# Page loads of a decoder step: one register load per four pages, page groups dealt 3:3:2 over three queues

## The reference, cut to what matters

```python
def dsa_sample(q, k, v, qi, ki, wi, cache_k, cache_v, cache_kidx, page_table, layer):
    ki_past = cache_kidx[layer, page_table].reshape(B, past, IDX_DIM)     # 8 x 32 pages of 128 x 64
    score = indexer_scores(qi, wi, concat([ki_past, ki], 1))              # sum_h w_h * relu(q_h . k)
    score = where(arange(L) <= pos_q, score, -inf)
    _, idx = lax.top_k(score, 256)
    ks, vs = rows idx of cache_k / cache_v by page_table, or of the new k / v   # pages of 128 x 2 x 64
    return sparse_attend(q, ks, vs, idx <= pos_q)                         # softmax over the kept keys
```

## Time and profile before

| What | us |
|---|---|
| median of 3 runs | 3424.85 |
| the profiled execution itself | 3424.24 |
| its span, first to last instruction | 3422.6 |
| index stage, first to last page transpose (L1911) | 1475.6 to 1560.7 |
| sample attention, first key transpose (L2531) to the last value matmul (L2586) | 2099.0 to 2334.9 |
| PE busy over the span | 2926.7 (86%) |
| POOL busy over the span | 315.7 (9%) |

### The profile page before, as it was taken

How to read it: one execution, slowest core, us unless ns; L and a number is a source line. 1 busy time by engine, 2 the same in 40 slices (tenths; PEclk the granted TensorE clock), 3 DMA queues, 4 the chain that set the end, 5 groups by cost and what they waited for, 6 DMA issues and landing times. The chain is left out here.

```text
span 3422.6 us, 45282 instructions
## 1 busy us (share of the span) xinstructions
PE 2926.7 (86%) x17508; PEld 2637.4 (77%) x17508; DVE 1499.2 (44%) x2239; ACT 871.9 (25%) x1350; POOL 315.7 (9%) x502
## 2 busy tenths in 40 slices
PE   7999999998599999677775686766969999999986
PEld 6999999998397899535775353446859999999984
DVE  3323233322545788357775674331342222233325
ACT  2111111110314577113443343321131111111102
POOL 0000000000000000043222003551000000000000
PEclk8999999999799999579998797888979999999998
DMA  3111111110121222142001003543011111111101
GB/s 116 38 50 38 45 42 43 37 49 6 54 66 38 64 70 89 52 108 53 27 24 60 35 1 87 150 130 121 12 58 41 43 43 44 44 44 38 46 10 53
DMA packets 258005, 185.86 MB, mean 54 GB/s; under 512 B 60191, under 2 KB 236527, under 8 KB 257814
## 3 DMA queue, kind: packets, MB, share of 16 engines
q1 hardware_dynamic: 216630, 115.07, 11.8%
q0 software_dynamic: 22752, 61.87, 5.5%
q10 hardware_dynamic: 18432, 6.30, 0.7%
HBM read 156.96 MB, written 26.22 MB: 54 GB/s over the span
## 5 line engine op out<-in xcount | busy, mean ns | idle before, releaser
L310 DVE TENSOR_TENSOR ffn_hidden<-ffn_hidden,ffn_ps_b 128x1092 f32<-128x1092 f32 x44 | 56.9, 1292 | 406.2 <-PE ffn_ps_b L84 406.2
L293 DVE TENSOR_TENSOR ffn_lo_g<-ffn_raw_g,ffn_hi_g 128x1024 fp32r<-128x1024 f32 x44 | 53.9, 1225 | 344.5 <-ACT ffn_hi_g L258 344.5
L177 POOL DMA_DIRECT2D ffn_raw_d<-in_ffn_w_down x44 | 23.5, 533 | 1783.3 <-DVE ffn_lo_d L299 1576.6
L265 ACT ACTIVATE ffn_hi_d<-ffn_raw_d 128x1024 fp32r<-128x1024 f32 x44 | 46.5, 1058 | 549.0 <-PE ffn_ps_b L84 424.6
L280 ACT ACTIVATE ffn_h_hi<-ffn_hidden 128x1092 fp32r<-128x1092 f32 x44 | 49.2, 1119 | 502.4 <-DVE ffn_hidden L310 502.4
L84 PE MATMUL ffn_ps_a<-mixer_mix_hi,ffn_hi_g 128*128 128x364 f32 x528 | 118.9, 334 | 42.6 <-DVE ffn_lo_g L293 30.1
L84 PE MATMUL ffn_ps_a<-ffn_h_hi,ffn_hi_d 128*128 128x364 f32 x528 | 120.2, 337 | 22.6 <-DVE ffn_lo_d L299 18.1
L84 PE MATMUL ffn_ps_a<-first_x_hi,ffn_hi_g 128*128 128x364 f32 x528 | 118.5, 333 | 21.4 <-DVE first_res L322 12.5
L273 ACT ACTIVATE ffn_hidden<-ffn_ps_a 128x1092 f32<-128x1092 f32 x44 | 47.7, 1083 | 316.9 <-PE ffn_ps_a L84 316.9
L84 PEld LDWEIGHTS ffn_ps_a<-mixer_mix_hi,ffn_hi_g 128*128 128x128 f32 x528 | 92.1, 190 | 45.9 <-DVE ffn_lo_g L293 30.6
L84 PE MATMUL ffn_ps_a<-ffn_h_hi,ffn_lo_d 128*128 128x364 f32 x528 | 118.3, 332 | 0.0
(11 more groups left out here) (566 smaller groups left out, 7139.5 us busy)
## 6 DMA issues: line engine op xcount, KB each, us to landing
ffn_raw_g<-in_ffn_w_gate SPq DMA_DIRECT2D x44, 512.0 KB, 3.7
ffn_raw_u<-in_ffn_w_up SPq DMA_DIRECT2D x44, 512.0 KB, 3.7
ffn_raw_d<-in_ffn_w_down POOLq DMA_DIRECT2D x44, 512.0 KB, 3.7
proj_raw<-in_w_in SPq DMA_DIRECT2D x22, 512.0 KB, 3.8
ats_k_raw<-in_cache_k POOLq DMA_DIRECT2D x128, 64.0 KB, 2.2
ats_v_raw<-in_cache_v POOLq DMA_DIRECT2D x128, 64.0 KB, 2.1
scratch_qkv<-proj_stage POOLq DMA_DIRECT2D x12, 544.0 KB, 3.0
delta_cur<-scratch_qkv SPq DMA_DIRECT2D x8, 768.0 KB, 5.4
```

The costliest lines, as they stand in the source:

```text
L177: eng.dma_start(dst, src).then_inc(raw_in[kind], 16)
L265: act.activation(d_hi[:, k, :], raw["d"][:, :], ACT.Copy).then_inc(whi_done["d"], 1)
L293: dve.tensor_tensor(lo[kind][:, :], raw[kind][:, :], hi[kind][:, :].bitcast(F32), ALU.subtract).then_inc(wlo_done[kind], 1)
L310: dve.tensor_tensor(hid, hid, ps_b[:, :, 0:SL], ALU.mult).then_inc(mul_done, 1)
```

## The change

`load_page` becomes `load_pages`: one register load brings the numbers of the four pages of one sample in a step, and four DMAs follow, all from one engine. What one engine loads is therefore a group of four pages, two groups to a step. In the index stage the groups go round SP, POOL, ACT (22, 21 and 21 of 64). In the attention the table `owner` repeats every four steps, shifted by one step for the values; over four steps, keys and values together, SP and POOL load six groups each and ACT four. PE waits only for engines that load into the buffer at hand. Data, buffers, sizes of the DMAs and the computation stay as they are.

```diff
-def load_page(eng, cache, pages, slot, dst, sem):
-    page = eng.value_load(pages[0:1, bass.ds(slot, 1)])
-    eng.dma_start(dst, cache[0, bass.ds(page, 1)].rearrange("o p ... -> (o p) ...")).then_inc(sem, 16)
+def load_pages(nc, eng, engine, cache, pages, slot, dst, sem):
+    _, numbers = nc.values_load_multi_w_load_instructions(pages[0:1, slot:slot + 4], engines=(engine,))
+    for g, page in enumerate(numbers):
+        eng.dma_start(dst(g), cache[0, bass.ds(page, 1)].rearrange("o p ... -> (o p) ...")).then_inc(sem, 16)
...
-    parts = {"sp": [(0, 0), (0, 1), (0, 2)], "pool": [(0, 3), (1, 0), (1, 1)], "act": [(1, 2), (1, 3)]}
+    turns = ("sp", "pool", "act")
...
-            if n >= bufs:
+            mine = [b2 for b2 in range(2) if turns[(2 * n + b2) % 3] == who]
+            if mine and n >= bufs:
                 eng.wait_ge(s["turned"], n - bufs + 1)
-            for b2, g in parts[who]:
-                load_page(eng, cache_kidx, pages, (p * 2 + b2) * PAGES + (i + h * rows_i) * 4 + g,
-                          raw[:, n % bufs, g, b2 * HD:(b2 + 1) * HD], s[f"raw_in_{who}{n % bufs}"])
+            for b2 in mine:
+                load_pages(nc, eng, engine, cache_kidx, pages, (p * 2 + b2) * PAGES + (i + h * rows_i) * 4,
+                           lambda g: raw[:, n % bufs, g, b2 * HD:(b2 + 1) * HD], s[f"raw_in_{who}{n % bufs}"])
...
-    parts = {"sp": [(0, 0), (0, 1), (0, 2)], "pool": [(1, 0), (1, 1), (1, 2), (1, 3)], "act": [(0, 3)]}
+    owner = {0: ("sp", "sp", "act", "sp"), 1: ("act", "pool", "pool", "pool")}
...
-        def load_k(eng, who, n):
+        def load_k(eng, engine, who, n):
+            mine = [b2 for b2 in range(2) if owner[b2][n % 4] == who]
...
-        def load_v(eng, who, m):
+        def load_v(eng, engine, who, m):
+            mine = [b2 for b2 in range(2) if owner[b2][(m + 1) % 4] == who]
```

More of the change, by code:

```diff
@@ L1871, in index_sample, with load_step @@
         block = ctx.enter_context(nc.Block())
-        def load_step(eng, who, n):
+        def load_step(eng, engine, who, n):
             i, p, h = steps[n]
-            if n >= bufs:
+            mine = [b2 for b2 in range(2) if turns[(2 * n + b2) % 3] == who]
+            if mine and n >= bufs:
                 eng.wait_ge(s["turned"], n - bufs + 1)
-            for b2, g in parts[who]:
-                load_page(eng, cache_kidx, pages, (p * 2 + b2) * PAGES + (i + h * rows_i) * 4 + g,
-                          raw[:, n % bufs, g, b2 * HD:(b2 + 1) * HD], s[f"raw_in_{who}{n % bufs}"])
+            for b2 in mine:
+                load_pages(nc, eng, engine, cache_kidx, pages, (p * 2 + b2) * PAGES + (i + h * rows_i) * 4,
+                           lambda g: raw[:, n % bufs, g, b2 * HD:(b2 + 1) * HD], s[f"raw_in_{who}{n % bufs}"])
         @block.sync
@@ L1883, in _ @@
             for n in range(total_steps):
-                load_step(sp, "sp", n)
+                load_step(sp, mybir.EngineType.SP, "sp", n)
         @block.gpsimd
@@ L1888, in _ @@
             for n in range(total_steps):
-                load_step(pool, "pool", n)
+                load_step(pool, mybir.EngineType.Pool, "pool", n)
         @block.tensor
@@ L1905, in turn @@
             def turn(n):
-                for who, which in parts.items():
-                    pe.wait_ge(s[f"raw_in_{who}{n % bufs}"], (n // bufs + 1) * 16 * len(which))
+                for who in turns:
+                    groups = [b2 for m in range(n % bufs, n + 1, bufs) for b2 in range(2)
+                              if turns[(2 * m + b2) % 3] == who]
+                    if groups:
+                        pe.wait_ge(s[f"raw_in_{who}{n % bufs}"], len(groups) * 64)
                 if n >= 2:
@@ L1957, in _ @@
             for n in range(bufs):
-                load_step(act, "act", n)
+                load_step(act, mybir.EngineType.Activation, "act", n)
             act.wait_ge(s["new_dotted"], 1)
@@ L1968, in _ @@
                 if n + bufs < total_steps:
-                    load_step(act, "act", n + bufs)
+                    load_step(act, mybir.EngineType.Activation, "act", n + bufs)
                 if n in cut_at:
@@ L2475, in half @@
             return slice(b2 * HD, (b2 + 1) * HD)
-        def load_k(eng, who, n):
-            if n >= bufs:
+        def load_k(eng, engine, who, n):
+            p, c = divmod(n, chunks)
+            mine = [b2 for b2 in range(2) if owner[b2][n % 4] == who]
+            if mine and n >= bufs:
                 eng.wait_ge(s["turned1"], n - bufs + 1)
[L2480 to L2483, removed]
@@ L2485, in load_v @@
-        def load_v(eng, who, m):
-            if m >= bufs:
-                eng.wait_ge(s["v_used"], m - bufs + 1)
[L2488 to L2493, removed]
+            for b2 in mine:
+                load_pages(nc, eng, engine, cache_k, pages, (p * 2 + b2) * PAGES + c * 4,
+                           lambda g: k_raw[:, n % bufs, b2, g, :], s[f"k_in_{who}{n % bufs}"])
@@ new lines, in load_v, with load_all @@
+        def load_v(eng, engine, who, m):
+            p, c = divmod(m, chunks)
+            mine = [b2 for b2 in range(2) if owner[b2][(m + 1) % 4] == who]
+            if mine and m >= bufs:
+                eng.wait_ge(s["v_used"], m - bufs + 1)
+            for b2 in mine:
+                load_pages(nc, eng, engine, cache_v, pages, (p * 2 + b2) * PAGES + c * 4,
+                           lambda g: v_raw[:, m % bufs, b2, g, :], s[f"v_in_{who}{m % bufs}"])
+        def load_all(eng, engine, who):
@@ L2494, in load_all @@
             for n in range(bufs):
-                load_k(eng, who, n)
+                load_k(eng, engine, who, n)
             for it in range(total + lag):
                 if it + bufs < total:
-                    load_k(eng, who, it + bufs)
+                    load_k(eng, engine, who, it + bufs)
                 if it < bufs:
-                    load_v(eng, who, it)
+                    load_v(eng, engine, who, it)
                 if bufs <= it - lag + 3 < total:
-                    load_v(eng, who, it - lag + 3)
+                    load_v(eng, engine, who, it - lag + 3)
@@ L2504, in pages_in @@
         def pages_in(pe, kind, n):
-            for who in parts:
-                pe.wait_ge(s[f"{kind}_in_{who}{n % bufs}"], (n // bufs + 1) * 16 * len(parts[who]))
+            shift = 0 if kind == "k" else 1
+            for who in ("sp", "pool", "act"):
+                groups = [b2 for m in range(n % bufs, n + 1, bufs) for b2 in range(2)
+                          if owner[b2][(m + shift) % 4] == who]
+                if groups:
+                    pe.wait_ge(s[f"{kind}_in_{who}{n % bufs}"], len(groups) * 64)
@@ L2511, in _ @@
                 sp.dma_start(q[:, j, :], q_in[j, :, PROMPT:NT]).then_inc(s["q_in"], 16)
-            load_all(sp, "sp")
+            load_all(sp, mybir.EngineType.SP, "sp")
         @block.gpsimd
         def _(pool):
-            load_all(pool, "pool")
+            load_all(pool, mybir.EngineType.Pool, "pool")
         @block.tensor
@@ L2658, in _ @@
             for n in range(bufs):
-                load_k(act, "act", n)
+                load_k(act, mybir.EngineType.Activation, "act", n)
             for it in range(total + lag + 3):
@@ L2667, in _ @@
                 if it + bufs < total:
-                    load_k(act, "act", it + bufs)
+                    load_k(act, mybir.EngineType.Activation, "act", it + bufs)
                 if it < bufs:
-                    load_v(act, "act", it)
+                    load_v(act, mybir.EngineType.Activation, "act", it)
                 if bufs <= it - lag + 2 < total:
-                    load_v(act, "act", it - lag + 2)
+                    load_v(act, mybir.EngineType.Activation, "act", it - lag + 2)
                 p, c = divmod(it - lag - 2, chunks)
```

## The result

The changed kernel takes 3327.92 us (median of 4 runs, 3322.04 to 3333.44) against 3423.86 us before on the same chip: ratio 0.9717, 95% interval 0.9697 to 0.9736. The profiled execution is the slowest of the four (3333.44 us, span 3331.7).

| us | before | after |
|---|---|---|
| index stage | 95.5 | 84.1 |
| sample attention | 237.9 | 143.1 |
| all the rest of the span | 3089.2 | 3104.5 |

The account below looks back on a forecast made before the run. POOL's page issue loop was taken to bound the sample attention; -66.5 us there and -7.5 in the index stage, -74 on 3424.24, with the median 0.6 above, gave 3351 us, range 3322 to 3380 (own case 3338 to 3362).

Parts of the forecast that it names:

- POOL's issue loop was the bound: Sample attention before the change: POOL's issuing, 0.902 us a page over 256 pages, was said to be the stage.
- L: Register load of four page numbers, once per group in both stages: put at 0.85 us, between 0.29 and 1.15.
- the upper bound: Load of four page numbers priced as four single loads: 1.15 us, or 1.04 for four fetches in turn.
- The rest of a page: POOL's cost per page without the register load, arithmetic, dispatch and DMA: 0.615 us, said to stay.
- the rival of the cheap load: Load of four near 0.29 us, PE becomes the attention's bound: -91 there, index stage -9, 3325 us; chance 0.22.
- both pass in full: Savings of index stage and sample attention, -74 us together, reach the total whole because both stages end in a barrier.
- PE's clock as a rival: Attention: 10 of 20 middle steps stay at the low clock, 7.3 us instead of 5; 3374 us, chance 0.10.
- ACT's longer issuing: Attention: ACT goes from 51 to 94 us of issuing, covered by its idle time; nothing charged, 2 us if uncovered.
- Stalls of four DMAs in a row: Four DMAs from one queue held up, SP group 7.7 us: 3555 us, a loss from 0.84 us mean issue; chance 0.03.
- Index stage: Index stage as a whole: -8.9 from DVE's waiting and +1.4 at ACT's start, together -7.5 us.
- The -8.9 for DVE: Index stage: DVE ends last, and of its 12.9 us of waiting 4 stay, saving 8.9 us.
- The +1.4 at ACT's start: Index stage start: ACT issues 20 pages ahead of `ixs_rel_new` in 14.7 us against 13.27, costing 1.4 us on the path.

Follow-up runs that it names:

- the widths: Changed kernel with POOL loading eight numbers per group, ACT five, SP four begun one place early plus its last number by itself; 3348.24 us.
- the run without late pages: Changed kernel with attention pages loaded only for the first four steps and those buffers reused afterwards; 3320.61 us, ratio 0.9685.
- the repetition: Meant as the attention change alone, but built as the changed kernel in both stages, so nothing differed from it; 3328.52 us, ratio 0.9707.
- the sharing alone: Changed kernel with its new sharing of groups, but four single register loads in each group instead of one load of four; 3371.47 us, ratio 0.9835.

## Why the prediction was right in its sign and 23 us off in its size

- **POOL's issue loop was the bound: shown.** Two different ways of shortening it alone, fewer groups (48 x 3.61 = 173) and a shorter group (64 x 2.69 = 172), gave stages of 176.9 and 179.6, each as long as POOL's loop with its standstill. With both (129) the stage is 143.1 and no longer follows the loop.
- **The step that failed is the size of L.** The forecast took 0.85 for the load of four; it measured 0.318, 0.298 and 0.309. The fault was in reading the upper bound as near: that 0.25 of a single load is fetching was inferred from the arithmetic row, and that four fetches would come one after another was assumed. As the widths showed, this holds for four numbers that don't start at a multiple of four (0.867, almost the 0.85), and `cut_pages` starts every group at one. The rest of a page was sized a little high as well, 0.615 against (2.69 - 0.318) / 4 = 0.59. So POOL's group took 2.69 instead of 3.31 us, and of the 0.62 between them 0.53 are L.
- **The Trainium skill's rule on L** ("Runtime: NRT & Kernel Launch", section "Instruction fetch mechanics", about 200 ns a register even in bulk, said of loads from HBM) agrees with the loads of two and three numbers (0.49 to 0.52 and 0.67) and with the shifted four (0.867), and not with the four of this kernel, 0.03 above one; the measurement decides.
- **What followed is the rival of the cheap load** (3325), which had a chance of 0.22; the forecast's own range of 3338 to 3362 was missed. PE became the floor with steps of 3.66. The rival had the last value matmuls at 2242, and they are at 2232.68. Most of that is where the stage begins: POOL's first page came at 2086.33, and the rival had counted from the 2093.75 of before. From there it forecast 148 us and 146 were measured: 40.2 against 40.0 to step 11, 79.4 against 78.2 for the 20 steps after that, and 26.8 against 30.4 for the values alone, at a clock of 1.00 where the rival had gone by a row at 0.80. That PE is the floor of the middle is shown by the run without late pages; at the stage's two ends pages still cost some 6 us.
- **The total is nearer to the forecast than its parts.** The two stages gave 106 us in the profile after and 100 in the repetition, where the forecast had 74; the median fell by 96. All eight traces with an edit have 2 to 15 us more outside of the two stages than the one trace of before has, so the traces do not bear out that "both pass in full". Whether a shorter stage costs time elsewhere, or the one trace of before is short there by chance, stays open. With the 106 alone the time would have been 3318, below the stated range; that it lies inside is in part luck.
- **PE's clock as a rival did not come.** It was 1.00 through the middle, where steps took 3.66 us and not the 5 of the rival's condition. Such steps were seen in two experiments: at 5.7 us a step the clock was 0.86 with two of twelve steps with transposes of the low level (the sharing alone), and with SP as the bound it was 0.93. The rival had set 10 of 20 steps. In both runs the stage was still as long as the issue loop with its waits.
- **ACT's longer issuing is covered**, as forecast: ACT is busy 30.58 of 60 us and PE's step does not feel it.
- **Stalls of four DMAs in a row: rare.** SP's page DMAs have a median of 0.333 us in the attention; seven of 192 took 0.87 to 1.76. The mean is 0.37, far below the 0.84 at which this rival turns into a loss. DMA share rose to 0.86, not 0.68, because the stage became shorter still; landings grew from 2.2 to 3.1 us without a cost in the middle.
- **Index stage: -11.4 instead of -7.5**, and -9.4 and -8.2 in the two other traces of the same stage. The -8.9 for DVE was near: its waits for transposes fell from 12.9 us to 4.3 (1490 to 1549). The +1.4 at ACT's start did not come, since 20 pages with cheap loads take 12.40 us, less than the 13.27 of 16 before. And that start was on the path only in part: 7.5 us less of it gave 2.5 to 5.7 in the stage and nothing clear in the time. With single loads the stage lost the whole gain (97.3), with the activation 16.9 us behind the first matmul instead of 13.1. DVE waited 21.8 us for transposes from 1475 to 1562 there, 8.2 of them in one wait right behind that activation; which engine's pages the other transposes lacked was not separated.

## What to carry to other kernels

When one engine issues all of a stage's small transfers, its loop (pages times the time of one) is the stage, and both fewer pages per engine and fewer instructions per page shorten it until the next bound; put a number on that next bound first, because two measures that gain 61 and 58 us alone gave 95 together. Read page numbers four at a time, in loads that start at a multiple of four, and look in the trace for the duration of each width used. When a term's bounds lie far apart and no row shows it, state both outcomes and which engine binds in each, as the total jumps where the bound changes.

## What the runs showed of the hardware that was not expected

- A register load from SBUF takes, in us by count of 4-byte numbers: one 0.27 to 0.29, two 0.49 to 0.52, three 0.67, four from a multiple of four 0.30 to 0.32, four from elsewhere 0.87, five 0.54 and eight 0.565 (both from a multiple of four). Five from one place before a multiple of four took 1.127 (one load).
- At a DMA share of 0.86 and 249 GB/s the pages of this stage landed 3.1 us after their issue instead of 2.2, and PE's step was the same 3.66 us as with a share of 0.01.
